# One of two products of P with V moved behind the projections and the scores of its half step, in a hybrid attention layer on one Trainium2 core

## The chip, the cores and the metric

The kernel runs on one core of a Trainium2 chip. Its time is the device time of one execution in microseconds, and less is better. TensorE (PE in the rows; its weight loads stand as PEld) does the matmuls, VectorE (DVE) and ScalarE (ACT) the elementwise work, GpSimd (POOL) and SyncE (SP) issue most of the transfers. Each engine works through its own list of instructions in order, and semaphores make it wait for the others.

## The reference, cut to what matters

```python
# one layer on 1024 prompt frames and 64 new frames of a stream with 1024 cached frames
h  = rms_norm(x, g_attn)
z  = h @ w_in                       # columns split into FoX q/k/v/forget, Diff q/k/v, two gates
# FoX attention: 8 heads of 64, causal
s  = q @ k.T / 8 + (cumsum(logf)[q] - cumsum(logf)[k])
oA = softmax(s) @ v
# Diff attention: 4 heads, two 64-wide maps, values 128 wide
oB = (softmax(s1) - lam * softmax(s2)) @ v
x1 = x + (sigmoid(gA) * (oA @ w_oa) + sigmoid(gB) * (subln(oB) @ w_ob)) @ w_out
y  = x1 + (silu(a) * b) @ w_down    # a, b: causal conv of width 3 over rms_norm(x1) @ w_up
```

The change lies in the FoX attention, in the product `softmax(s) @ v`.

## The kernel before

All data are 32 bit wide. A product is made of three matmuls of high and low parts (the projections and the scores), or of two for P with V, where P and V are split into 16-bit high and low parts.

The attention stage runs eight **units**. The first four are of kind A (two FoX heads each, called the maps m = 0 and 1), the last four of kind B (one Diff head with its two maps). A unit also holds, as **jobs**, the projections of the next unit's Q, K and V (`Q0` to `K2`), its own gates (`G00` to `G12`), sums of squares (`SQ`, `SK`), transposes (`VT`, `KT`, `KC`, `OT`) and column maxima (`VS0`, `CS0`). A job with a number is one third of the tokens (364, 364 or 360 columns). A projection is 24 matmuls on TensorE.

Within a unit, nine query tiles follow each other in the order `TILES = [7, 6, 5, 8, 4, 3, 2, 1, 0]`. Tile i has i + 1 blocks of 128 keys, and tile 8 holds the 64 new frames with 1088 keys. I call what the plan does for the n-th of them **step n**; it has two halves. `unit_plan` writes the order of all this as one list, and every engine walks the same list and takes its own part of each item:

- `("S", i, c)`: scores of tile i, chunk c of up to 512 keys, both maps. TensorE writes them to `psS` (three banks, used in turn), VectorE adds the bias, takes the minimum and writes `sc` (line 1629, semaphore `s_d`).
- `("E", i)`: ScalarE's exponentials of tile i (line 1239).
- `("T", i, m)`: TensorE turns P of map m into `psT` (L895), ScalarE writes its high half `pT_h`, VectorE the low half `pT_l` (L1427, semaphore `tl_d`).
- `("AV", i, m)`: TensorE multiplies P with V into the single bank `psO`; VectorE then adds its two halves into `o_tm` (L1666, semaphore `o_d`). A product may start only when the reduction of the product before it has read `psO`: `pe.wait_ge(S["o_d"], g - 1)`.
- `("J", name)`: a job. ScalarE takes its bank off. `L`, `CB`, `VA`, `VB`, `RD`, `SCALE` and `SPLIT` are further work of VectorE: the low half of a weight block (`w_l`, L1422), the scale of the cached V (six small instructions, L1501 to L1508), the maximum and the scale of V, the reciprocal of the roots, the normalization of q and k (L1484), the low halves of q and k.

For kind A, step n reads in the plan of before: T(i,0); the product of the last step's map 1; the exponentials; `flush` (waiting VectorE work); the jobs of the first half; T(i,1); the first score chunk of the tile after the next; the product of map 0, AV(i,0); `flush`; the jobs of the second half; the second score chunk. The next step begins with its T and then AV(i,1). The jobs of the second halves are, for n = 0 to 8: SQ0; CS0 and SQ1; SQ2; K1 and SK0; SK2 and VT0; G00; G01; KC0; G11. A second score chunk stands in the steps 0, 1 and 2 only.

Of the kernel before, what the change touches and what calls it, by code (L numbers as in the profile page):

```python
# [67 lines left out]
def unit_plan(kind, nxt):  # L68

    if nxt:  # L70
        slots = {"first": ["Q0"], "second": ["Q1"], "third": ["Q2"], (0, 0): ["V0"], (0, 1): ["SQ0"], (1, 0): ["V1"],
# [4 lines left out]
    else:  # L76
        slots = {"first": ["G00"], "second": ["G01"], "third": ["G02"], (0, 0): ["G10"], (1, 0): ["G11"], (1, 1): ["CS0"],
                 (2, 0): ["G12"], "end": ["OT0", "OT1", "OT2"]}
    at_once = {"CS0": [("CB",)]}
    then = {"CS0": [("VC",)], **({"KT2": [("H", "FIRST")], "VT2": [("ROOT",)]} if nxt else {})}  # L80
    later = {"VS0": [("VB",)], **({"V2": [("VA",)], "VT2": [("RD",)], "G02": [("SCALE",)], "KT2": [("L", "FIRST")]} if nxt else {})}
    for a, b in WEIGHTS_AFTER[nxt].items():
        then[a] = then.get(a, []) + [("H", b)]
        later[a] = later.get(a, []) + [("L", b)]
    acts, pending = [], []
    plan = [("GS",)]

    def jobs(slot):
        for n in slots.get(slot, []):
            plan.append(("J", n))  # L90
            plan.extend(at_once.get(n, []))
            acts.extend(then.get(n, []))
            pending.extend(later.get(n, []))

    def act_flush():
        plan.extend(acts)
        acts.clear()

    def flush():
        act_flush()  # L100
        plan.extend(pending)
        pending.clear()

    def scores(n, c):
        if n < NT and c < len(KEY_CHUNKS[TILES[n]]):
            plan.append(("S", TILES[n], c))

    maps = 2 if kind == "A" else 1
    scores(0, 0)
    jobs("first")  # L110
    scores(0, 1)
    jobs("second")
    plan.append(("E", TILES[0]))
    act_flush()
    scores(1, 0)
    if kind == "B":
        plan.append(("C", TILES[0]))
    flush()
    jobs("third")
    scores(1, 1)  # L120
    for n, i in enumerate(TILES):
        plan.append(("T", i, 0))
        if n:
            plan.append(("AV", TILES[n - 1], maps - 1))
        split_tail = n + 1 < NT and len(KEY_CHUNKS[TILES[n + 1]]) == 3
        if n + 1 < NT and not split_tail:
            plan.append(("E", TILES[n + 1]))
        if kind == "B" and n > 1:
            plan.append(("SQO", TILES[n - 2]))
        if kind == "B" and 4 <= n < NT - 1:  # L130
            plan.append(("C", TILES[n + 1]))
        flush()
        jobs((n, 0))
        if split_tail:
            scores(n + 1, 2)
        if kind == "A":
            plan.append(("T", i, 1))
        if split_tail:
            plan.append(("E", TILES[n + 1]))
        if kind == "B" and n < 4 and not split_tail:  # L140
            plan.append(("C", TILES[n + 1]))
        act_flush()
        scores(n + 2, 0)
        if kind == "A":
            plan.append(("AV", i, 0))
        elif split_tail:
            plan.append(("C", TILES[n + 1]))
        flush()
        if nxt and n == 8:
            plan.append(("SPLIT", 0, 1))  # L150
        jobs((n, 1))
        scores(n + 2, 1)
        if n == 0:
            plan.append(("CA",))
    plan.append(("AV", TILES[-1], maps - 1))
    flush()
    if kind == "B":
        plan.append(("SQO", TILES[-2]))
        plan.append(("SQO", TILES[-1]))
    plan.append(("OFIN",))  # L160
    if nxt:
        plan.append(("SPLIT", 2))
    jobs("end")
    assert not pending and not acts
    return plan
# [35 lines left out]
def build(nc, ins, outs):  # L201
# [193 lines left out]
    def hold(e, name, value, own):  # L395
# [4 lines left out]
        e.sem_inc(S[own], 1)  # L400

    PLANS = {(k, n): unit_plan(k, n) for k, n in (("A", True), ("B", True), ("B", False))}
    INDEX = {kn: plan_index(p) for kn, p in PLANS.items()}
    JOBS1 = PROLOGUE_JOBS
# [1460 lines left out]
```

How the kernel before makes its waits and increments, by code:

```python
    def wait(e, name, value):  # L389
        if isinstance(value, int) and value <= 0:
            return
        e.wait_ge(S[name], value)
# [1 line left out]
    def hold(e, name, value, own):  # L395
        if isinstance(value, int) and value <= 0:
            return
        e.wait_ge(S[name], value)
        e.sem_inc(S[own], 1)
# [75 lines left out]
        def spread_roots(count, n, meanwhile=None):  # L476
            sp.wait_ge(S["pj_d"], count)
            sp.dma_start(ms_scr[0:2], sqq[0:2, :]).then_inc(S["ms_o"], 16)
            sp.dma_start(ms_scr[2:4], sqk[0:2, :]).then_inc(S["ms_o"], 16)
            sp.wait_ge(S["ms_o"], n * 32 + 32)
            sp.dma_start(meansq[:], ms_scr.rearrange("r t -> (r t)").rearrange("(p c) -> p c", p=P)
                         ).then_inc(S["ms_i"], 16)
            if meanwhile:
                load_w(*meanwhile)
            sp.wait_ge(S["rt_d"], n + 1)
            sp.dma_start(rt_scr.rearrange("r t -> (r t)").rearrange("(p c) -> p c", p=P), root[:]
                         ).then_inc(S["rt_o"], 16)
            sp.wait_ge(S["rt_o"], n * 16 + 16)
            for x, dst in enumerate((sqq, sqk)):
                for h in range(2):
                    sp.dma_start(dst[DH * h:DH * h + DH, :], rt_scr[2 * x + h:2 * x + h + 1].broadcast_to([DH, T])
                                 ).then_inc(S["rt_i"], 16)
# [63 lines left out]
    @block.gpsimd  # L557
# [11 lines left out]
        pool.memset(half_ones[DH:P, DH:P], 1.0 / DH).then_inc(S["cst"], 1)  # L569
        pool.wait_ge(S["cst"], 5)
        pool.memset(maskf[:], 0.0).then_inc(S["msk"], 1)
```

## Time and profile before

| | |
|---|---|
| median of 3 runs | 2012.92 us (2007.97 to 2017.12) |
| the profiled execution | 2014.17 us, span 2012.6 us |
| TensorE busy | 1879.1 us, 93% of the span |
| VectorE busy | 1011.8 us, 50% |
| ScalarE busy | 759.9 us, 38% |
| granted TensorE clock, mean | 0.976 of full speed |
| the four A units | 132 to 568 us of the span, some 109 us each |

A duration in a row is that of one instruction, or of several alike (x2). What stands in square brackets at its end is how long the engine had been idle before it, and which instruction released it. The clock column (PEclk) is the granted TensorE clock as a share of full speed, 1.00 being 2.4 GHz and 0.50 being 1.2 GHz.

### The profile page before, as it was taken

Reading aid. Unit: us, or ns where it says so; the run is one execution under the profiler, and the core shown is the slowest. Engines: PE = TensorE matmul, PEld = TensorE weight load, DVE = VectorE, ACT = ScalarE, POOL = GpSimd, SP = SyncE. Lnnn points to the kernel's source line nnn. Section 1 sums busy time; section 2 is a strip of 40 time slices with the busy share of each in tenths; the row PEclk is TensorE's granted clock in tenths of the full one; section 3 lists DMA queues with packets and bytes.
Section 4 is the critical chain, followed back from the end, with each engine's and each line's share of the span. In section 5 each row is a group of like instructions: output and inputs, shape, how many; then the busy total and the mean of one; then the engine's idle time right before and its main releaser. Section 6 shows DMA issues by size and latency. Waiting matters only on the chain.

```text
span 2012.6 us, 32531 instructions
## 1 busy us (share of the span) xinstructions
PE 1879.1 (93%) x11943; PEld 1744.0 (87%) x11943; DVE 1011.8 (50%) x1962; ACT 759.9 (38%) x1335; POOL 109.2 (5%) x183
## 2 busy tenths in 40 slices
PE   5979999999999999996899999999999999999987
PEld 4868888888887878785899989999999999999986
DVE  4535454545465556556653365542555345535542
ACT  3535455554555555454311244421232122212221
POOL 3110101000010000000000000000000000000011
PEclk9979999999999999998899999999999999999999
DMA  6140513224231213133342211111111111021121
GB/s 215 32 129 16 166 29 113 81 60 135 56 98 46 96 55 97 33 109 110 111 139 98 87 32 42 39 47 50 38 46 39 44 42 48 27 61 32 42 70 62
DMA packets 153954, 144.63 MB, mean 72 GB/s; under 512 B 8008, under 2 KB 134066, under 8 KB 153888
## 3 DMA queue, kind: packets, MB, share of 16 engines
q1 hardware_dynamic: 135296, 78.29, 14.0%
q0 software_dynamic: 18592, 65.46, 9.2%
q8 instruction: 42, 0.69, 0.1%
q14 instruction: 24, 0.20, 0.0%
HBM read 112.61 MB, written 31.11 MB: 71 GB/s over the span
## 4 chain that ended last, share of the span: by engine, by line
PE 82%; DVE 6%; ACT 4%; issue 4%; DMA 2%; DVEq 0%; ACTq 0%; POOL 0%; SPq 0%; POOLq 0%
PE bank L707 45%; PE psS L707 19%; PE psO L707 11%; PE psT L895 2%; PE psT L707 1%; DMA gate<-gate_scr 1%; ACT pT_h L1054 1%; PE bank L767 1%; ACT sc L1239 0%; PE psT L891 0%; PE psT L736 0%; DVE sc L1646 0%; PE bank L819 0%; DMA x_tm<-in_x_prompt 0%; DVE m_a L1727 0%
## 5 line engine op out<-in xcount | busy, mean ns | idle before, releaser
L707 PE MATMUL bank<-xn_hi,w_h 128*128 128x364 f32 (+1 forms) x952 | 327.1, 344 | 18.5 <-DVE xn_lo L1422 11.7
L707 PE MATMUL bank<-xn_lo,w_h 128*128 128x364 f32 (+1 forms) x952 | 315.9, 332 | 0.0
L707 PE MATMUL bank<-xn_hi,w_l 128*128 128x364 f32 (+1 forms) x952 | 315.5, 331 | 0.0
L1054 ACT ACTIVATE w_h<-wraw 128x1024 fp32r<-128x1024 f32 x133 | 139.5, 1050 | 214.7 <-PE psO L707 205.4
L707 PEld LDWEIGHTS bank<-xn_hi,w_h 128*128 128x128 f32 x952 | 182.1, 191 | 32.1 <-issue 22.5
L1422 DVE TENSOR_TENSOR w_l<-wraw,w_h 128x1024 fp32r<-128x1024 f32 x133 | 162.4, 1221 | 52.7 <-ACT w_h L1054 52.7
L707 PEld LDWEIGHTS bank<-xn_lo,w_h 128*128 128x128 f32 x952 | 182.1, 191 | 0.0
L707 PEld LDWEIGHTS bank<-xn_hi,w_l 128*128 128x128 f32 x952 | 181.6, 191 | 0.0
L1361 ACT ACTIVATE ct<-u,vecs 128x1090 f32<-128x1090 f32 x44 | 57.2, 1300 | 328.1 <-DVE u L1786 328.1
L707 PE MATMUL psS<-x_l,w_h 128*128 128x364 f32 (+1 forms) x528 | 173.5, 329 | 0.0
L707 PE MATMUL psS<-x_h,w_l 128*128 128x364 f32 (+1 forms) x528 | 173.5, 329 | 0.0
L707 PE MATMUL psS<-x_h,w_h 128*128 128x364 f32 (+1 forms) x528 | 173.4, 328 | 0.0
L707 PE MATMUL bank<-g_h,w_h 128*128 128x364 f32 x352 | 118.2, 336 | 9.2 <-DVE g_l L1422 5.2
L1427 DVE SCALAR_TENSOR_TENSOR pT_l<-psT,pT_h 128x1024 f16<-128x1024 f32 (+8 forms) x72 | 54.5, 757 | 142.5 <-ACT pT_h L1054 142.5
L707 PE MATMUL bank<-x_h,w_h 128*128 128x364 f32 x352 | 116.3, 330 | 7.8 <-DVE x_l L1761 4.3
L1239 ACT ACTIVATE sc<-sc,smin 128x1024 f32<-128x1024 f32 (+5 forms) x144 | 116.8, 817 | 1.8 <-DVE smin L1629 1.8
L707 PE MATMUL bank<-g_h,w_l 128*128 128x364 f32 x352 | 116.3, 331 | 0.0
L707 PE MATMUL bank<-g_l,w_h 128*128 128x364 f32 x352 | 116.2, 330 | 0.0
L707 PE MATMUL bank<-x_l,w_h 128*128 128x364 f32 x352 | 115.7, 329 | 0.0
L707 PE MATMUL bank<-x_h,w_l 128*128 128x364 f32 x352 | 115.7, 329 | 0.0
L707 PEld LDWEIGHTS psS<-x_h,w_h 128*128 128x128 f32 x528 | 99.2, 188 | 0.0
L707 PEld LDWEIGHTS psS<-x_h,w_l 128*128 128x128 f32 x528 | 99.2, 188 | 0.0
(337 smaller groups left out, 4068.7 us busy)
## 6 DMA issues: line engine op xcount, KB each, us to landing
wraw<-in_w_up SPq DMA_DIRECT2D x44, 512.0 KB, 3.7
wraw<-in_w_in SPq DMA_DIRECT2D x41, 512.0 KB, 3.8
gate<-gate_scr POOLq DMA_DIRECT2D x16, 544.0 KB, 4.5
wraw<-in_w_down SPq DMA_DIRECT2D x16, 384.0 KB, 3.4
wraw<-in_w_down SPq DMA_DIRECT2D x16, 320.0 KB, 3.0
x_scr<-xT POOLq DMA_DIRECT2D x8, 544.0 KB, 4.3
cum_s<-c_scr POOLq DMA_DIRECT2D x8, 544.0 KB, 7.6
sqq<-rt_scr SPq DMA_DIRECT2D x16, 272.0 KB, 4.0
```

The source lines that it names most:

```text
L707: return pe.matmul(out, w, x, start=first, stop=last, **kw)
L767: r = pe.transpose(bank[0:n, P * j:P * j + P], src[:, P * t:P * t + n], ident[:])
L895: r = pe.transpose(out[:, P * kb:P * kb + P], src[:, P * kb:P * kb + P], ident[:])
L1054: return act.activation(out, in_, ACT.Copy, **kw)
L1239: act.activation(sc[x][m][:, 0:n], sc[x][m][:, 0:n], ACT.Exp, bias=smin[:, low:low + 1], scale=-1.0, accum_out=den[x][:, m:m + 1]).then_in ...
L1361: act.activation(ct[h][:], ub[h][:, 2:TU], ACT.Identity, scale=taps[2][:, bass.ds(b, 1)], bias=cbias[:, bass.ds(b, 1)]).then_inc(S["ct_a"], 1)
L1422: return dve.tensor_tensor(out, in_, high_of(high), ALU.subtract)
L1427: return dve.scalar_tensor_tensor(out, in_, scale, high, ALU.mult, ALU.subtract)
```

## The change

AV(i,0) of kind A leaves its place between the first score chunk and the `flush`, and stands behind the second half's jobs and the second score chunk. AV(i,0) and AV(i,1) are then separated by the T of the next step alone, and in step 8 by nothing. The combination item `C` of kind B keeps its place, and the B units are unchanged. No instruction is added or taken away.

```diff
         act_flush()
         scores(n + 2, 0)
-        if kind == "A":
-            plan.append(("AV", i, 0))
-        elif split_tail:
+        if split_tail and kind == "B":
             plan.append(("C", TILES[n + 1]))
         flush()
         if nxt and n == 8:
             plan.append(("SPLIT", 0, 1))
         jobs((n, 1))
         scores(n + 2, 1)
+        if kind == "A":
+            plan.append(("AV", i, 0))
         if n == 0:
             plan.append(("CA",))
```

TensorE in step 7 (tile 1), before: T(1,1), the product of map 0 (`psO`, four rows), the job KC0 (`kc_tm`), T(0,0), the product of map 1.

```order
L895 MATMUL psT<-ident,sc 128x128 x2
L707 MATMUL psO<-v_hl,pT_h 128x128
L707 MATMUL psO<-v_hl,pT_l 128x64
L707 MATMUL psO<-v_hl,pT_h 128x128
L707 MATMUL psO<-v_hl,pT_l 128x64
L393 REGISTER_ALU
L810 ISA
L812 MATMUL bank<-ident,kc_tm 128x128 x4
L882 REGISTER_ALU
L895 MATMUL psT<-ident,sc 128x128
L707 MATMUL psO<-v_hl,pT_h 128x128
L707 MATMUL psO<-v_hl,pT_l 128x64
```

The same place now:

```order
L895 MATMUL psT<-ident,sc 128x128 x2
L393 REGISTER_ALU
L810 ISA
L812 MATMUL bank<-ident,kc_tm 128x128 x4
L707 MATMUL psO<-v_hl,pT_h 128x128
L707 MATMUL psO<-v_hl,pT_l 128x64
L707 MATMUL psO<-v_hl,pT_h 128x128
L707 MATMUL psO<-v_hl,pT_l 128x64
L882 REGISTER_ALU
L895 MATMUL psT<-ident,sc 128x128
L707 MATMUL psO<-v_hl,pT_h 128x128
L707 MATMUL psO<-v_hl,pT_l 128x64
```

The first product has moved behind KC0, and only one transpose is left between the two products.

VectorE at the same place, before: `pT_l` of T(1,1), the reduction of AV(1,0), then the normalization of q and k, and the low half of the cached keys of KC0.

```order
L1427 SCALAR_TENSOR_TENSOR pT_l<-psT,pT_h 128x256
L1657 RECIPROCAL norm_a<-small 128x1
L1666 TENSOR_REDUCE o_tm<-psO 128x64
L1482 REGISTER_ALU
L1484 SCALAR_TENSOR_TENSOR zq<-zq,small,sqq 128x1088
L1484 SCALAR_TENSOR_TENSOR zk<-zk,small,sqk 128x1088
L1523 REGISTER_ALU
L1422 TENSOR_TENSOR kc_l<-bank,kc_h 128x512
```

The same place now:

```order
L1427 SCALAR_TENSOR_TENSOR pT_l<-psT,pT_h 128x256
L1657 RECIPROCAL norm_a<-small 128x1
L1482 REGISTER_ALU
L1484 SCALAR_TENSOR_TENSOR zq<-zq,small,sqq 128x1088
L1484 SCALAR_TENSOR_TENSOR zk<-zk,small,sqk 128x1088
L1523 REGISTER_ALU
L1422 TENSOR_TENSOR kc_l<-bank,kc_h 128x512
L1666 TENSOR_REDUCE o_tm<-psO 128x64
```

The reduction has moved behind three large VectorE instructions.

VectorE in step 1 (tile 6), before, from the reduction of AV(6,0) to the first score chunk behind the scale:

```order
L1666 TENSOR_REDUCE o_tm<-psO 128x64
L1433 REGISTER_ALU
L1422 TENSOR_TENSOR w_l<-wraw,w_h 128x1024
L1601 REGISTER_ALU
L1501 TENSOR_REDUCE scl<-peaks 128x1
```

And now, the end of the same stretch: the last instructions of the scale, the second chunk of the scores of both maps, the reduction.

```order
L1507 TENSOR_SCALAR scl<-scl 128x1
L1508 TENSOR_SCALAR scl<-scl 128x1
L399 REGISTER_ALU
L1629 ISA sc,smin<-psS,cum_s,smin 128x512
L1629 ISA smin 128x1
L399 REGISTER_ALU
L1629 ISA sc,smin<-psS,cum_s,smin 128x512
L1629 ISA smin 128x1
L1666 TENSOR_REDUCE o_tm<-psO 128x64
```

The reduction stood ahead of the weight's low half, and now stands behind it, the scale and two score chunks. The lists of ScalarE, GpSimd and SyncE are unchanged.

## Rows read from the trace of the kernel before

**Rows 1.** Busy time by stretch: second A unit; us, busy by engine (count), clock, DMA

```profile
241.40:350.20 108.80, 104.64 (x790) 91.00 (x789) 54.81 (x147) 56.10 (x112) 8.52 (x13) 1.00 0.29 90
```

**Rows 2.** TensorE's waits in that unit: us in total, times, longest

```profile
PE psO L707 <- DVE o_tm L1666: 1.8, 2, 1.1
```

**Rows 3.** Timeline, TensorE, step 0: start us, us, instruction

```profile
264.66 0.23 PE L707 MATMUL psO<-v_hl,pT_h 128*128 128x128 f16 x1
...
265.44 0.78 PE L707 MATMUL bank<-sqq,half_ones 128*2 128x364 f32 x2
266.87 0.39 PE L707 MATMUL psS<-k_h,q_h 64*128 64x256 f32 x2 [0.65 <-DVE smin L1629]
```

**Rows 4.** Timeline, VectorE, step 1

```profile
277.43 0.29 DVE L1666 TENSOR_REDUCE o_tm<-psO 128x64 f32<-128x128 f32 x1
277.63 1.22 DVE L1422 TENSOR_TENSOR w_l<-wraw,w_h 128x1024 fp32r<-128x1024 f32 x1
...
281.24 0.95 DVE L1427 SCALAR_TENSOR_TENSOR pT_l<-psT,pT_h 128x768 f16<-128x768 f32 x1
```

**Rows 5.** Timeline, TensorE, step 1: the product AV(6,1) begins

```profile
278.56 0.22 PE L707 MATMUL psO<-v_hl,pT_h 128*128 128x128 f16 x1
```

**Rows 6.** Timeline, VectorE, steps 2 and 4

```profile
287.92 0.29 DVE L1666 TENSOR_REDUCE o_tm<-psO 128x64 f32<-128x128 f32 x1
288.12 1.21 DVE L1513 TENSOR_REDUCE scl<-zv 128x1 f32<-128x1024 f32 x1
...
289.79 0.75 DVE L1427 SCALAR_TENSOR_TENSOR pT_l<-psT,pT_h 128x576 f16<-128x576 f32 x1
...
311.31 0.28 DVE L1666 TENSOR_REDUCE o_tm<-psO 128x64 f32<-128x128 f32 x1
311.51 1.22 DVE L1422 TENSOR_TENSOR w_l<-wraw,w_h 128x1024 fp32r<-128x1024 f32 x1
312.70 0.69 DVE L1427 SCALAR_TENSOR_TENSOR pT_l<-psT,pT_h 128x512 f16<-128x512 f32 x1
```

**Rows 7.** Timeline, TensorE, steps 2 and 4: AV(5,1) and AV(4,1) begin

```profile
288.99 0.23 PE L707 MATMUL psO<-v_hl,pT_h 128*128 128x128 f16 x1
...
311.76 0.22 PE L707 MATMUL psO<-v_hl,pT_h 128*128 128x128 f16 x1
```

**Rows 8.** Timeline, VectorE, step 7

```profile
332.35 0.27 DVE L1666 TENSOR_REDUCE o_tm<-psO 128x64 f32<-128x128 f32 x1
332.53 1.34 DVE L1484 SCALAR_TENSOR_TENSOR zq<-zq,small,sqq 128x1088 f32<-128x1088 f32 x1
...
335.66 0.28 DVE L1427 SCALAR_TENSOR_TENSOR pT_l<-psT,pT_h 128x128 f16<-128x128 f32 x1
```

**Rows 9.** Timeline, TensorE, step 7: T(0,0), and AV(1,1) begins

```profile
331.81 0.27 PE L895 MATMUL psT<-ident,sc 128*128 128x128 f32 x1
332.76 0.22 PE L707 MATMUL psO<-v_hl,pT_h 128*128 128x128 f16 x1 [0.68 <-DVE o_tm L1666]
```

**Rows 10.** Timeline, VectorE, step 8: the reduction of AV(0,1)

```profile
345.27 0.28 DVE L1666 TENSOR_REDUCE o_tm<-psO 128x64 f32<-128x128 f32 x1
```

**Rows 11.** Timeline, TensorE, step 8: AV(0,1) begins

```profile
344.30 0.23 PE L707 MATMUL psO<-v_hl,pT_h 128*128 128x128 f16 x1
```

**Rows 12.** Timeline, TensorE, step 6: AV(2,0) begins

```profile
322.08 0.22 PE L707 MATMUL psO<-v_hl,pT_h 128*128 128x128 f16 x1 [1.10 <-DVE o_tm L1666]
```

**Rows 13.** TensorE's waits in the fourth A unit

```profile
PE psO L707 <- DVE o_tm L1666: 0.7, 1, 0.7
```

**Rows 14.** Timeline, TensorE, two waits in B units

```profile
610.57 0.34 PE L891 MATMUL psT<-ident,sc 64*128 64x64 f32 x1 [2.15 <-DVE sc L1646]
...
941.95 0.33 PE L895 MATMUL psT<-ident,sc 128*128 128x128 f32 x1 [1.76 <-DVE sc L1646]
```

**Rows 15.** Busy time and clock around these two waits (columns as in Rows 1)

```profile
609.00:619.00 10.00, 8.43 (x44) 7.92 (x45) 5.50 (x12) 2.74 (x7) 0.00 (x0) 0.66 0.00 0
936.00:944.00 8.00, 4.78 (x46) 3.55 (x45) 6.55 (x22) 4.81 (x17) 0.00 (x0) 1.00 0.38 153
```

## The prediction

> **What bounds the kernel now.** I read the busy time by stretch first. Of the 108.80 us of the second A unit TensorE is busy for 104.64 at full clock, VectorE for 54.81 [rows 1]. So TensorE's own list is the path, and every microsecond in which it waits counts. The list of TensorE's waits says how little that is now: 1.8 us on the reduction of `psO`, in two waits [rows 2]. I then read the timelines of the nine steps beside each other, since the change moves one product and one reduction in each step, and the question is who waits at the new place. Times below are those of the second unit; in the other three the steps follow each other with nearly the same distances, with one exception, which is named.
>
> **The rule of the change.** TensorE's work stays the same. What changes is (a) what fills a wait of TensorE, and (b) where the reduction of AV(i,0) stands in VectorE's list. For (b): AV(i,1) may start only when that reduction is done, and now only one T lies between the two products. VectorE works in order, so AV(i,1) waits for everything in VectorE's list ahead of the reduction. From the end of a reduction to the start of the waiting product there pass 0.14 us (332.35 + 0.27 = 332.62 to 332.76) [rows 8, 9]. A reduction that is taken away lets its follower start 0.20 us earlier (277.43 to 277.63) [rows 4].
>
> **Step 0.** Before, AV(7,0) runs from 264.66 to 265.44 (0.78 us), then SQ0, then 0.65 us of waiting until VectorE has read the first score chunk and `psS` is free, at 266.87 [rows 3]. VectorE's side is the same now, so the second chunk still starts at 266.87; the product no longer fills the wait and is worked off behind it: **+0.78**. The reduction is ready in time there.
>
> **Step 1.** The reduction stood at 277.43. Now the weight's low half, the scale and both score chunks come first; they end where `pT_l` starts now, 281.24, less the 0.20 that they move up: 281.04. The reduction ends at 281.04 + 0.28 = 281.32, and AV(6,1) starts at 281.46 in place of 278.56 [rows 4, 5]: **+2.90**, of which some 2.2 us is TensorE idle in one piece, since AV(6,0) itself (0.68 us) now lies there too.
>
> **Step 2.** Ahead of the reduction now stand the maximum of V and the short score chunks, to 289.79 less 0.20: 289.59. With 0.28 and 0.14 AV(5,1) starts at 290.01 in place of 288.99 [rows 6, 7]: **+1.02**.
>
> **Step 4.** The weight's low half goes first, to 312.70 less 0.20: 312.50, so AV(4,1) starts at 312.92 in place of 311.76 [rows 6, 7]: **+1.16**. **Step 3** has a whole projection (K1) ahead of AV(8,0), VectorE is idle by then, and T(4,0) is long enough for the reduction: 0.
>
> **Steps 5 and 6.** Here the change helps: AV(2,0) waited 1.10 us for the reduction of AV(3,1) [rows 12], and now G01 runs in that wait. Against it stand two short T, of three and two transposes, which don't quite cover the new reductions: I take 0.2 and 0.25 us, and add 0.15 for T and AV(3,0) at their new places. Together **-0.5**. The fourth A unit has only 0.7 us of such waits, the one of step 7 [rows 13], so the 1.10 isn't there to win: +0.4.
>
> **Step 7.** Ahead of the reduction now stand the normalizations of q and k (1.34 us each) and `kc_l`, to 335.66 less 0.20: 335.46. With 0.28 and 0.14 AV(1,1) starts at 335.88 in place of 332.76 [rows 8, 9]: **+3.12**. This is the longest new wait: T(0,0) stands where it stood, and TensorE is idle from about 332.1 to 335.9, of which 0.68 us was there before.
>
> **Step 8.** AV(0,0) comes behind G11, right before AV(0,1). Its reduction stands behind the low halves of q and k, where now that of AV(0,1) starts at 345.27; AV(0,1) starts at 345.27 + 0.28 + 0.14 = 345.69 in place of 344.30 [rows 10, 11]: **+1.39**. What queues behind each of these waits on TensorE is the next projection (V1, V2, K0, G10, G12), and ScalarE and the next unit wait for that in turn. The transfers hang on events that move with TensorE or come earlier relative to it, and I cost them at nothing; were one uncovered, the cost would be that of the transfer's tail, under 1 us.
>
> **Sum of the waits.** 0.78 + 2.90 + 1.02 + 1.16 - 0.5 + 3.12 + 1.39 = 9.87 us in each of three units, 10.8 in the fourth: 40.4 us. An error of 10% in each wait would be 4 us.
>
> **The clock.** In the B units TensorE waits 2.15 us in one piece (one such row stands for four, 2.05 to 2.15), and behind each the clock falls to its lower level, 1.2 GHz. Over the ten microseconds from 609 the mean clock is 0.66, which is 10 x 0.34 = 3.4 us of work lost [rows 14, 15]. A wait of 1.76 us at 941.95 lies in a stretch with clock 1.00 [rows 14, 15], and so do all waits of up to 1.10 us in the A units. The new waits of step 7 (3.1 us and more, with only a transpose and a short product around it) and step 1 (2.2 us, with products and transposes close by) are on the wrong side of these rows. The bounds are no fall at all (0) and a fall at all eight places (8 x 3.4 = 27 us). The same 2.15 us needn't always suffice, so I take five of the eight, and 3 us for each, since part of the slow stretch may lie in the wait itself: **+15 us**.
>
> The Trainium skill (TensorE: Matmul & The Clock Gate, the table "Why this matters for your kernels") sets the idle gap that brings the lower clock higher than the 2.15 us of rows 14. By that rule step 1 would keep its clock and step 7 alone would lose it, for 4 x 3 = 12 us, a time of 2065; the rows decide for more than that.
>
> **The time.** The profiled execution took 2014.17 us: 2014.17 + 40.4 + 15 = 2069.6. It stands 1.25 us above the median of the three runs, 2012.92, so I predict **2068 us**, 2.7% slower.
>
> **Rivals.**
> - *The waits alone.* TensorE waits as summed, and the clock holds. For it: the A units hold 1.00 with their waits of up to 1.10 us, and the 1.76 us wait held. Against it: four of four waits of 2.05 us or more had a fall behind them. 2012.9 + 40.4 = 2053 us. Chance 0.22.
> - *A fall at all eight places.* 2053 + 27 = 2080 us. Chance 0.13; step 1's wait is just about as long as the B units', but among more work.
> - *The waits are partly absorbed.* If a delay of TensorE in one step is given back in the next, because VectorE has caught up, half of the 40 us could go: about 2033 us. Against it: the timelines show each step's VectorE work released by TensorE of the same step, so a delay is carried on. Chance 0.09.
> - *Faster.* One mechanism: VectorE reaches the moved reductions before TensorE has done the next T, so AV(i,1) never waits, and what remains is the waits on `psO` that go: 1.8 us in each of three units and 0.7 in the fourth [rows 2, 13], some 6 us: 2007 us. It decides at the point where what stands ahead of the reduction is shorter than a T of 0.3 to 1 us; the rows show 1.2 to 3.6 us there in steps 1, 2, 4 and 7 [rows 4, 6, 8]. Chance 0.02.
> - *The plan's order isn't what sets the engines' order.* Then 2013 us. The instruction lists show the move on TensorE and VectorE, so 0.02.
>
> **How the numbers follow.** The forecast (2061 to 2076 us) has the remaining 0.52. The range is to leave out no more than 2 in 10. From below it takes in the waits alone with 4 us less for mis-sized ones and a microsecond of scatter: 2048. From above, the eight falls with 3 us to spare: 2083. A measurement of this kernel tells about 0.5%, 10 us, from no change. Faster by more: 0.02. Within: 0.02. Slower by more: 0.96.
>
> **What would show it.** In the trace of the changed kernel TensorE's waits on `psO` should be some 9 us in each A unit where they were 1.8, the longest over 3 us in step 7, right behind `zq`, `zk` and `kc_l`, and one over 2 us in step 1. The wait of 1.10 us at AV(2,0) should be gone. The wait on the scores in step 0 should be about 1.4 us in place of 0.65. The A units should be some 119 us long, more where the clock column falls under 1.00 behind steps 1 and 7. I would be wrong if AV(i,1) starts right behind the T (then the waits aren't of this kind), or if clock falls come behind waits of 1.2 us too (then more than 2083), or if the B units' own falls change with the shifted times, which is worth up to four times 3.4 us in either direction.

## The result

| | before | changed |
|---|---|---|
| median | 2011.76 us | 2060.0 us |
| runs | 2007.97 to 2017.12 | 2052.09 to 2062.36 |
| the profiled execution | 2014.17 us | 2062.36 us |

The changed kernel takes 1.0225 times as long, with a 95% interval of 1.0181 to 1.0268. One execution of the changed kernel took 3030.01 us at a mean granted clock of 0.567: it is left out of the runs and the ratio above, the median of 2060.0 is over all four, and that of the other three is 2057.64, 45.9 us over the kernel before. Timed again in a later comparison, beside 11 runs of the kernel before, it took 2059.83 us, 1.0243 times as long (1.0225 to 1.0261), 47.3 us more. The forecast was 2068 us with a range of 2048 to 2083.

The page of the changed kernel, its two lines on engines and clock first. TensorE has the same 11943 matmuls:

```profile
PE 1890.3 (92%) x11943; PEld 1751.3 (85%) x11943; DVE 1013.9 (49%) x1962; ACT 760.8 (37%) x1335; POOL 109.2 (5%) x183
...
PEclk9989999999999999999699999999999999999999
```

The second A unit, by busy time (columns as in [rows 1]) and by TensorE's waits (us in total, times, longest):

```profile
254.20:375.30 121.10, 107.84 (x790) 93.28 (x789) 55.40 (x147) 56.35 (x112) 8.51 (x13) 0.97 0.26 81
```

```profile
PE psO L707 <- DVE o_tm L1666: 8.7, 6, 3.8
PE psS L707 <- DVE smin L1629: 3.2, 3, 1.4
```

The unit has grown from 108.80 to 121.10 us with the same 790 matmuls. The waits on the reduction have gone from 1.8 us in two [rows 2] to 8.7 us in six, those on the scores from 1.2 to 3.2 us, in three each time. That TensorE's busy time has grown too, from 104.64 to 107.84 us, is the clock: 0.97 where it was 1.00.

Now the places of [rows 3 to 12] in the changed kernel. The timeline rows have the start in us, the duration, the instruction and, in brackets, the idle time before it. First TensorE where it has waited in the steps 0, 1, 2 (two rows), 4, 6, 7 and 8:

```profile
279.70 0.39 PE L707 MATMUL psS<-k_h,q_h 64*128 64x256 f32 x2 [1.44 <-DVE smin L1629]
295.01 0.22 PE L707 MATMUL psO<-v_hl,pT_h 128*128 128x128 f16 x1 [2.16 <-DVE o_tm L1666]
303.91 0.33 PE L707 MATMUL psS<-k_h,q_h 64*128 64x128 f32 x2 [0.97 <-DVE smin L1629]
306.48 0.22 PE L707 MATMUL psO<-v_hl,pT_h 128*128 128x128 f16 x1 [0.43 <-DVE o_tm L1666]
331.74 0.22 PE L707 MATMUL psO<-v_hl,pT_h 128*128 128x128 f16 x1 [0.94 <-DVE o_tm L1666]
346.00 0.22 PE L707 MATMUL psO<-v_hl,pT_h 128*128 128x128 f16 x1 [0.22 <-DVE o_tm L1666]
355.19 0.26 PE L707 MATMUL psO<-v_hl,pT_h 128*128 128x128 f16 x1 [3.80 <-DVE o_tm L1666]
369.36 0.22 PE L707 MATMUL psO<-v_hl,pT_h 128*128 128x128 f16 x1 [1.15 <-DVE o_tm L1666]
```

Then VectorE in step 1 and in step 7, each up to the reduction:

```profile
290.96 1.22 DVE L1422 TENSOR_TENSOR w_l<-wraw,w_h 128x1024 fp32r<-128x1024 f32 x1
...
293.23 0.75 DVE L1629 CUSTOM_DVE_ANT_0 sc<-psS,cum_s,smin 128x512 f32<-128x512 f32 x1
293.90 0.74 DVE L1629 CUSTOM_DVE_ANT_0 sc<-psS,cum_s,smin 128x512 f32<-128x512 f32 x1
294.58 0.28 DVE L1666 TENSOR_REDUCE o_tm<-psO 128x64 f32<-128x128 f32 x1
```

```profile
351.65 1.33 DVE L1484 SCALAR_TENSOR_TENSOR zq<-zq,small,sqq 128x1088 f32<-128x1088 f32 x1
352.90 1.35 DVE L1484 SCALAR_TENSOR_TENSOR zk<-zk,small,sqk 128x1088 f32<-128x1088 f32 x1
354.17 0.68 DVE L1422 TENSOR_TENSOR kc_l<-bank,kc_h 128x512 fp32r<-128x512 f32 x1
354.77 0.28 DVE L1666 TENSOR_REDUCE o_tm<-psO 128x64 f32<-128x128 f32 x1
```

In step 7 TensorE has had its product done since 351.25 and is idle from 351.39, VectorE works through three large instructions, reduces at 354.77, and TensorE goes on at 355.19. The same is seen in step 1: the reduction ends at 294.86 and the product starts at 295.01, 0.15 us later. It is 0.15 us in all 24 waits of this kind in the four A units. The wait of 1.10 us ahead of AV(2,0) [rows 12] is gone.

Last the clock. I call a stretch in which the granted clock is at its lower level, 0.50, a **fall**. The stretches behind step 1 of the first unit and behind step 7 of the first and second, and two waits in B units:

```profile
173.00:178.00 5.00, 4.49 (x28) 4.52 (x29) 3.04 (x8) 0.51 (x2) 0.00 (x0) 0.66 0.23 71
235.00:240.00 5.00, 5.00 (x24) 4.93 (x22) 0.00 (x0) 0.20 (x1) 0.00 (x0) 0.66 0.00 0
354.00:359.00 5.00, 3.81 (x18) 3.84 (x19) 1.60 (x6) 0.00 (x0) 0.00 (x0) 0.66 0.00 0
658.00:666.00 8.00, 5.86 (x41) 5.50 (x40) 6.23 (x17) 3.38 (x10) 0.00 (x0) 0.79 0.00 0
763.00:773.00 10.00, 7.98 (x43) 7.47 (x44) 5.88 (x15) 2.98 (x8) 0.00 (x0) 0.66 0.00 0
```

A fall in an A unit takes 5 x 0.34 = 1.7 us of work here, not the 3.4 of [rows 15]. In the B units both sizes occur now: 8 x 0.21 = 1.7 and 10 x 0.34 = 3.4.

**Step by step**, what was added in the second unit. Each is the growth of a distance on TensorE, from the start of the next projection to that of a later one; steps 4 and 5 are parted at the start of AV(4,1). What a projection ran longer at the lower clock is taken out and stands in the last row:

| part | forecast | measured |
|---|---|---|
| step 0 | +0.78 | +0.72 |
| step 1 | +2.90 | +2.91 |
| step 2 | +1.02 | +1.17 |
| step 3 | 0 | -0.13 |
| step 4 | +1.16 | +1.10 |
| steps 5 and 6 | -0.5 | -0.60 |
| step 7 | +3.12 | +3.15 |
| step 8 | +1.39 | +1.42 |
| sum | 9.87 | 9.74 |
| clock | 3.75 | 2.53 |

The clock's part is that of the projections that ran longer behind steps 2 and 7: 1.39 and 1.14 us. (The forecast's 3.75 is its 15 us over four units.)

### The profile page after: what moved, and what is told of

The parts are those of the page before. It is cut to its first block, busy times and chain, and to the rows that moved or that the text cites. A ratio compares the mean times of both kernels' runs of the same rounds, so it can differ in the third digit from the quotient of the medians.

```text
span 2060.8 us, 32531 instructions
## 1 busy us (share of the span) xinstructions
PE 1890.3 (92%) x11943; PEld 1751.3 (85%) x11943; DVE 1013.9 (49%) x1962; ACT 760.8 (37%) x1335; POOL 109.2 (5%) x183
## 4 chain that ended last, share of the span: by engine, by line
PE 77%; DVE 9%; issue 5%; ACT 5%; DMA 3%; DVEq 0%; POOL 0%; ACTq 0%; SPq 0%; POOLq 0%
PE bank L707 43%; PE psS L707 17%; PE psO L707 11%; PE psT L895 2%; DMA gate<-gate_scr 2%; DVE sc L1629 1%; ACT pT_h L1054 1%; DVE w_l L1422 1%; DVE m_a L1727 1%; PE bank L767 1%; DVE q_l L1422 0%; PE psT L707 0%; DVE m_b L1727 0%; ACT w_h L1054 0%; ACT sc L1239 0%
## 5 line engine op out<-in xcount | busy, mean ns | idle before, releaser
L707 PE MATMUL psO<-v_hl,pT_h 128*128 128x128 f16 (+2 forms) x444 | 68.6, 249 | 35.9 <-DVE o_tm L1666 35.4
```

The source lines that it names most:

```text
L707: return pe.matmul(out, w, x, start=first, stop=last, **kw)
```

## The experiments

The theory: TensorE waits because the reduction that frees `psO` stands behind VectorE's heavy work, and its clock falls behind the longest of these waits. The rival: the loss lies in TensorE's own list, where the product no longer fills a wait.

Times of whole runs carry a part that has nothing to do with the change. In the profiled executions the first scores of the first unit start at 126.9 to 130.0 us, and the falls in the B units differ from one to the next. So beside each ratio stands the length of the **A stage** in the profiled execution, from that start of TensorE to the start of the multiplication that ends the fourth A unit on VectorE (L1685 in the kernel before). It isn't free of such parts either: each A stage begins at the lower clock, which lasts another 5.6 to 6.3 us in most of these executions, but 3.2 us in that of the kernel with its waits filled, which is worth 1.5 us of work to it.

| kernel | A stage, us | over before | median, us | before beside it |
|---|---|---|---|---|
| before | 432.05 | | | |
| changed | 480.98 | +48.9 | 2057.64 | 2011.76 |
| changed again | 480.64 | +48.6 | 2059.83 | 2012.49 |
| late on TensorE alone | 447.6 | +15.6 | 2022.04 | 2007.29 |
| late on VectorE alone | 488.4 | +56.4 | 2064.67 | 2007.29 |
| changed, waits filled | 471.8 | +39.8 | 2047.69 | 2007.29 |
| steps 1 and 7 only | 462.7 | +30.6 | 2042.76 | 2007.29 |
| all but 1 and 7 | 447.7 | +15.6 | 2029.18 | 2012.49 |

The whole change of the time lies in the A stage: it is 48.9 us longer, and the profiled executions differ by 48.2. Of the 48.9 us, 37.5 are TensorE idle and 11.4 are TensorE busy for longer with the same work.

### TensorE late, VectorE early, and the reverse

`unit_plan` gets an argument that says whether AV(i,0) is late. In the first of two runs VectorE walks the plan in which it is early and the other engines the one in which it is late; in the second it is the other way round. ScalarE's list is the same in both plans.

```diff
+        if kind == "A" and not (late):
+            plan.append(("AV", i, 0))
...
-        if kind == "A":
+        if kind == "A" and (late):
             plan.append(("AV", i, 0))
...
-            for it in U.plan:
+            for it in DVE_PLANS[U.kind, U.nxt]:
```

> TensorE walks the changed plan, VectorE alone walks the plan of before: the product AV(i,0) comes late, its reduction stands ahead of VectorE's other work as before. Theory (the loss is the reduction's place in VectorE's list): the waits of 2.2 us in step 1 and 3.8 us in step 7 are gone, and with them the clock falls. Left are the product that no longer fills a wait in steps 0, 1 and 2 (about 0.7 us each), 0.2 in step 4, -0.5 in steps 5 and 6, and in step 8, where VectorE now waits for the late product before it can start on the low halves of q and k, about 1.8: some 3.7 us for each A unit, so 15 us over the kernel before (near 2027). Rival (the loss is TensorE's own order, the product that no longer fills a wait): about as slow as the changed kernel, 2055 to 2062.

Measured: 2022.04 us beside 2007.29, 1.0084 times (1.0064 to 1.0103), 14.8 us. TensorE's waits in the second unit of this kernel, and VectorE at step 8:

```profile
PE psS L710 <- DVE smin L1632: 3.2, 3, 1.4
PE psO L710 <- DVE o_tm L1669: 1.4, 3, 0.7
```

```profile
346.12 0.29 DVE L1669 TENSOR_REDUCE o_tm<-psO 128x64 f32<-128x128 f32 x1 [3.45 <-PE psO L710]
...
350.19 1.36 DVE L1688 TENSOR_TENSOR o_tm<-o_tm,norm_a 128x1152 f32<-128x1152 f32 x1
```

The waits on `psO` are down from 8.7 to 1.4 us. The waits on the scores have stayed at 3.2 us, as they must if they come from the product that no longer fills them. At step 8 VectorE itself waits 3.45 us for the late product, ahead of the low halves of q and k. TensorE's next two distances grow by 0.74 and 0.94 us there, 1.7 together, and the expectation gave about 1.8 for it. The falls of steps 1 and 7 are gone, as expected; one other came, in step 2 of the third unit behind a wait of 0.97 us on the scores.

> The other half alone: TensorE walks the plan of before, VectorE alone the changed one, so the product stands where it stood and only its reduction comes late. Theory: AV(i,1) waits for VectorE's list as in the changed kernel: 0.7 + 2.9 + 1.0 + 1.2 + 3.1 + 1.4 = 10.3 us for each A unit, 41 in all, and some 8 to 10 us of clock falls: 2058 to 2064, as slow as the changed kernel. Rival (TensorE's order): near the kernel before, under 2025.

Measured: 2064.67 us, 1.0289 times (1.0268 to 1.031), 57.4 us. The waits in the second unit, and the product of step 1:

```profile
PE psO L710 <- DVE o_tm L1669: 11.3, 7, 3.8
PE psS L710 <- DVE smin L1632: 1.2, 3, 0.7
```

```profile
295.86 0.22 PE L710 MATMUL psO<-v_hl,pT_h 128*128 128x128 f16 x1 [2.75 <-DVE o_tm L1669]
```

This kernel leaves TensorE's list as it was before, and it is slower than the changed one. In step 1 it waits 2.75 us where the changed kernel waits 2.16, since AV(6,0) doesn't stand in that wait. The median is within the range that was expected, but over the kernel beside it the step is 57 us where 49 to 51 were expected: the waits are those of the expectation (the second unit is 123.0 us long where it was 108.8), and more falls came on top, nine in the A stage of the profiled execution, three of them with the larger loss of 3.4 us. Both rivals are out: the place of the reduction alone makes the kernel as slow as the whole change does, and the place of the product alone costs 15 us. The two don't add up (15 and 57 against 46 to 47), since a product that comes late fills part of the wait that a late reduction makes.

### The waits filled with work

Ahead of AV(6,1) and AV(1,1) TensorE runs 11 and 20 matmuls into a bank of `psS` that has been read. Their results are never used. The rest is the changed kernel.

```diff
+                    if U.kind == "A" and m == 1 and i in (1, 6):
+                        k = ITEMS if i == 1 else U.item[8, 0, 1]
+                        pe.wait_ge(S["s_d"], U.s0 + k)
+                        b = (k - 1) % 3
+                        for _ in range(20 if i == 1 else 11):
+                            mm(psS[:, 512 * b:512 * b + 364], ident_r[:], xn[0][:, 0, 0:364], True, True)
                     pe.wait_ge(S["tl_d"], g)
```

> The changed kernel with matmuls of no use ahead of AV(6,1) (11) and AV(1,1) (20) in each A unit, written to a free bank and never read; at 0.167 us each they take 1.8 and 3.3 us, less than the waits of 2.2 and 3.8 us that they stand in. Theory (of the 49 us some 9 are the clock, 1.1 to 1.4 us for each of seven falls): the waits on the reduction end at the same distance, the clock stays at 1.00 behind both steps, and the time is 8 to 10 us under the changed kernel, about 2050. Rival (the falls cost nothing beside the waits): same as the changed kernel within 2 us, in the A units' lengths too. Second rival (a fall costs 3 us, as I predicted): 20 us less.

Measured: 2047.69 us (2046.24 to 2050.11), 1.0209 times the kernel before beside it (1.0191 to 1.0228), where the changed kernel had 1.0225 and 1.0243. In microseconds over the kernel before: 40.4, against 45.9 and 47.3. Step 7 of the second unit:

```profile
341.93 3.58 PE L707 MATMUL psS<-xn_hi,ident_r 128*128 128x364 f32 x20
345.98 0.22 PE L707 MATMUL psO<-v_hl,pT_h 128*128 128x128 f16 x1 [0.47 <-DVE o_tm L1672]
```

The stretches around steps 1 and 7, in this kernel and then in the changed one:

```profile
282.00:300.00 18.00, 15.49 (x142) 13.00 (x143) 13.30 (x42) 8.26 (x16) 0.00 (x0) 1.00 0.11 29
340.00:356.00 16.00, 14.52 (x96) 13.46 (x95) 6.49 (x13) 6.08 (x14) 1.43 (x2) 1.00 0.12 33
```

```profile
291.00:309.00 18.00, 14.44 (x131) 12.05 (x130) 12.07 (x38) 8.39 (x15) 0.00 (x0) 0.94 0.11 29
350.00:366.00 16.00, 11.19 (x69) 10.25 (x68) 6.03 (x13) 5.62 (x13) 0.97 (x2) 0.89 0.12 33
```

The product still starts late, but the clock holds, in steps 1 and 7 of all four units. What is left, 40.4 us, is the sum of the waits as the prediction has it, 40.4. Two falls remained in this A stage, in step 2 of the third and fourth units, so the match is closer than it deserves. By the medians the clock's share is 5 to 7 us, less than the 8 to 10 expected, and the intervals of the ratios overlap (1.0191 to 1.0228, and 1.0225 to 1.0261). The traces are clearer: the A stage is 9.2 us shorter than that of the changed kernel, 1.5 of it by the clock at its start, which leaves 7.6 us for five falls fewer, some 1.5 each. The rival of 3 us for each fall, 20 us in all, is out, and so is that of no difference.

### The change in parts

AV(i,0) is late only where the step's number is in a set.

```diff
-        if kind == "A":
+        if kind == "A" and (n in (1, 7)):
             plan.append(("AV", i, 0))
```

> The change in steps 1 and 7 only, the other seven steps as before. Theory: 2.9 + 3.1 = 6.0 us of waits for each A unit, 24 in all, and about one to two falls a unit, 6 to 9 us: 2042 to 2046. Rival (every step costs about the same, two ninths of the whole): 2011.8 + 11 = 2023.

Measured: 2042.76 us, 1.0183 times (1.0166 to 1.02), 35.5 us over the kernel beside it. The A stage is 30.6 us longer, as expected (24 us of waits and 6 to 9 of falls; there were five falls). Two of nine steps carry 30.6 of 48.9 us there. The median lies in the range expected, but that was reckoned from the 2011.8 of the first comparison; over the 2007.29 of this comparison it is 3 to 5 us more than the sum of waits and falls, and none of that stands in the A stage.

The complement, `n not in (1, 7)`, ran beside the changed kernel once more:

> The changed kernel itself once more, on the chip of the three runs below, for their comparison. Both theories: 47 to 51 us over the kernel before.

> The change in all steps but 1 and 7. Theory: 0.7 + 1.1 + 1.1 - 0.6 + 1.4 = 3.7 us for each A unit, some 15 in all, plus 0 to 4 us for a few clock falls behind steps 2 and 3: 15 to 19 us over the kernel before. With the 35 us of steps 1 and 7 that makes the whole. Rival (the delays of one step are taken up by the waits of the next, so that the parts don't add up): under 8 us.

Measured: the changed kernel 2059.83 us (47.3 over before), the complement 2029.18, 1.0084 times (1.0065 to 1.0103), 16.7 us. In the A stage the parts add up to 30.6 + 15.6 = 46.2 us, the whole to 48.6 and 48.9. The remaining 2.5 us are in part one fall: the two parts had five and one in their A stages, the whole had seven of the small size, and the second time five small ones and one of 3.4 us. The rest is open. By the medians the parts make 35.5 + 16.7 = 52.2 us against 46 to 47, so the parts add up to the whole within some 5 us either way, and no better.

### What the finding is good for

If a wait costs its length and a fall behind it, the B units of the kernel before can be helped: each has a wait like the one of 2.15 us in [rows 14]. In the first three B units, 11 unused matmuls go ahead of the transposes of tile 8, into the bank that the next job will use.

```diff
+                if it[:2] == ("T", 8) and U.kind == "B" and U.nxt:
+                    pe.wait_ge(S["pj_d"], U.j0 + idx - 1)
+                    for _ in range(11):
+                        mm(bank_of(idx + 1, U)[:, 0:364], ident_r[:], xn[0][:, 0, 0:364], True, True)
```

> The kernel before with 11 matmuls of no use in the wait of 2.15 us ahead of the transposes of tile 8 in the first three B units, 1.8 us of work in a free bank. Theory (such a wait costs its length and the fall behind it, 1.7 or 3.4 us of work): the falls behind these three waits go, so 5 to 10 us under the kernel before. Rival (the falls come from something else in these units): no difference, within 2 us.

Measured: 2003.26 us (2001.89 to 2004.11) beside 2012.49 (2006.07 to 2017.01), 0.9951 times (0.9937 to 0.9965). The ten microseconds around each of the three places:

```profile
601.00:611.00 10.00, 9.11 (x69) 7.17 (x68) 8.01 (x22) 5.24 (x10) 0.00 (x0) 1.00 0.00 1
707.00:717.00 10.00, 9.64 (x70) 7.94 (x66) 7.25 (x19) 5.22 (x12) 0.00 (x0) 1.00 0.00 0
813.00:823.00 10.00, 9.79 (x71) 8.64 (x72) 6.87 (x20) 4.60 (x12) 0.00 (x0) 1.00 0.00 0
```

The clock was 0.66 at all three in the kernel before, over the ten microseconds from 609 [rows 15], 716 and 822, and is 1.00. The distances between the L1685 or L1701 of one unit and the next show the price: in the first two B units they are 3.0 and 2.9 us shorter, one fall of 3.4 us less in each. The third is 1.4 us shorter: the clock held in the filled wait, but a fall of 1.7 us came ahead of it, at 770.45, with no wait over 1.1 us close by. That makes 7.4 us. The 9.2 between the medians is more; the profiled execution also had 1.6 us less in the A stage, by the clock at its start, with which the filling has nothing to do.

The runs also lie closer together, 2.2 us against 11, so much of the scatter of the kernel before looks like falls that come in some executions and not in others; that is an inference from the two spreads.

> The same, with the change made in step 6 alone, where it took a wait of 1.10 us away in three of the four A units. Theory: 0.6 to 0.9 us more in each of three units, so 7 to 12 us under the kernel before. Rival: as the run before it or slower.

Measured: 2002.39 us, 0.9946 times (0.9931 to 0.9962), 10.1 us under. The 0.9 us to the run before it can't be told from nothing by the times. The trace shows it: TensorE's waits on `psO` in the second unit are 0.9 us, where [rows 2] has 1.8, and the second and third units are 107.99 and 107.94 us long where they were 108.88 and 108.82; the fourth, the one without the 1.10 us wait [rows 13], is 107.78 where it was 107.36, which the expectation had left out.

```profile
PE psO L709 <- DVE o_tm L1672: 0.9, 2, 0.7
```

**Not tried.** A second place for the product would take the waits away at their root, since AV(i,1) wouldn't need the reduction of AV(i,0). The kernel has given its banks to `psS` (three), `psT` (two), `psO` (one) and the jobs (two), so it would mean another layout, and no run here shows what that would be worth.

## Why the prediction was right, and where it wasn't

- **The rule** held: AV(i,1) waits for everything in VectorE's list ahead of the reduction. The two runs in which one engine alone took the change show it from both sides, 15 and 57 us. The 0.14 us from the reduction to the waiting product came out as 0.15 in all 24 waits.
- **The waits of steps 0 to 8** came out within 0.15 us of the forecast each, 9.74 us against 9.87 for the second unit. What made this work was that each new start was worked out from a row of VectorE on the same stretch, less 0.20 for the reduction that leaves and plus 0.28 and 0.14 for the reduction and the restart. Step 2's part has a different make-up than forecast: the wait on the scores grew from 0.35 to 0.97 us, and only 0.43 us is left to wait for the reduction.
- **Steps 5 and 6** gave the small gain, and the fourth unit didn't.
- **The transfers** were put at nothing, with "under 1 us" if one were uncovered. No run shows that figure; in the second unit of the changed kernel no wait of TensorE of 0.2 us or more ends on a transfer.
- **The clock** is the term that was mis-sized. The forecast had five falls at 3 us each, 15 us. There were seven in the A stage of the profiled execution (behind or in the wait of step 7 in all four units, behind step 1 in the first and third, in step 2 of the second), and together they cost what is left of the 48.9 us beside the 40.4 forecast for the waits, some 8.5 us, 1.2 each. (TensorE was busy for 11.4 us longer at the lower clock; the rest of that lay in time in which it would have waited anyway.) More falls than forecast, at less than half the price: the two errors partly cancel, and that is luck.
- **The step that failed** is "10 x 0.34 = 3.4 us of work lost", taken from one row of a B unit. That size is one of two, and the other, 1.7 us, is what twelve of the thirteen falls had in the A stages of the changed kernel's two profiled executions (all seven in the first, five of six in the second). Where a fall of 3.4 us was taken away, in the B units, it gave back 2.9 and 3.0 us, so "3 us for each" was right for that size. In the profiled execution the A stage is 48.9 us longer where 55.4 were forecast, and those 6.5 us are the larger part of why the median came 8 us under the forecast, or 10 by the three executions.
- **When the clock falls** was read from too short a stretch. The 1.76 us wait "lies in a stretch with clock 1.00", but that stretch ends at 944.00, and at 944.99, 3.0 us behind the wait, the clock fell (0.58 over the six microseconds from 944), with a wait of 1.54 us at its beginning. And the prediction would have been wrong "if clock falls come behind waits of 1.2 us too (then more than 2083)". One did, behind 0.97 and 0.43 us in step 2; it was one place of the four, and small, so the time stayed far under 2083.
- **The rivals.** "The waits alone" (2053) is refuted by the falls in the trace and by the filled waits, which took 7.6 us off the A stage. "All eight places" had a fall at six, and would have needed the larger loss as well. The absorbed waits, the faster case and the case of an unchanged order didn't show at all.
- **The Trainium skill** (TensorE: Matmul & The Clock Gate, "Why this matters for your kernels") warns of idle gaps of more than about 3 us. By that step 7 alone should lose the clock. Step 7 agrees, with 3.80 us and a fall in four of four units. Step 1 lost it too, in two of four units, behind waits of 2.17 us, and so did the B units of the kernel before, with waits of 2.05 to 2.15 us. The measurement decides.

## What to carry to other kernels

Moving a producer's work also moves the consumer's step that releases its buffer. With a single buffer the price is what stands ahead of that step in the consumer's list, and rows of the consumer's timeline gave it here within 0.15 us a step. A wait of the matmul engine costs more than its length once its clock falls behind it. If such a wait can't be removed, filling it with matmuls of no use got that part back here, at every place that was filled. A price that was read from one fall is to be checked against several.

## What the runs showed of the hardware

- In the changed kernel the clock fell in step 1 behind waits of 2.17 us in two of four units (2.16 us in the second and 2.11 us in the fourth had none), in step 7 with a wait of 3.80 us in four of four (in the second unit the fall began 0.57 us ahead of the wait's end), and once behind two shorter waits, 0.97 and 0.43 us in step 2, with products and transposes between them. Step 2 had a fall in other profiled executions too: once with the change in all steps but 1 and 7, once with the product alone late, twice with the waits filled, and three times with the reduction alone late, each time with no wait over 1 us in that step. With the reduction alone late, two of four waits of some 2.7 us had none.
- The waits of 2.05 to 2.15 us in the B units brought a fall in all four units of the kernel before and of the changed one. With the product alone late, two of these four waits had none (those that end at 622 and 725 us), and with the waits filled the one that ends at 753 us had none.
- In the A units and the first three B units every fall took 1.7 or 3.4 us of work (3.4 or 6.8 us at the lower level), and nothing between. The same place had 3.4 in the kernel before and 1.7 in the changed one (the first B unit). A fall of 1.7 us made the time 1.1 to 1.5 us longer, one of 3.4 us 2.9 to 3.0. The fourth B unit had one of 10.2 us at the lower level in the changed kernel, 5.1 us of work.
- 11 or 20 matmuls that write what nobody reads kept the clock at 1.00 through the wait and behind it, in eight places of the A units and three of the B units.
- From the end of VectorE's reduction to the start of the product that waits for it there pass 0.15 us, in all 24 waits of the changed kernel's A units.
